# Four of six key/value chunks as seven half products instead of eight

## The reference

```
kv = rms_norm(x1, g_kv) @ w_kv      # 640 x 2048 by 2048 x 3072
k, v = jnp.split(kv, 2, axis=-1)    # outputs, and used by layer 1
```

## Time and profile before

| | us |
|---|---|
| three runs: median (lowest, highest) | 2202.61 (2198.36, 2204.11) |
| the profiled execution, and its span | 2199.25, 2197.6 |
| PE, DVE, ACT, POOL busy | 2166.1, 1140.8, 880.5, 314.8 |
| out_a starts / kv starts / in_b starts (first matmul) | 821.0 / 1045.4 / 1380.8 |

### The profile page before, as it was taken

One profiled execution on the slowest core, in us unless ns is written; L12 is line 12 of the kernel. 1 busy time (PEld: TensorE's weight loads), 2 busy tenths in 40 slices (PEclk: granted clock), 3 DMA queues, 4 the chain that ended last, 5 costly groups with the idle time before them and its releaser, 6 DMA issues.

```text
span 2197.6 us, 33765 instructions
## 1 busy us (share of the span) xinstructions
PE 2166.1 (99%) x12524; PEld 1860.4 (85%) x12524; DVE 1140.8 (52%) x1972; ACT 880.5 (40%) x1701; POOL 314.8 (14%) x466
## 2 busy tenths in 40 slices
PE   8999999999999999999999999999999999999998
PEld 6888888888888998888788888888888888988887
DVE  5758988988745463224522222255555554663223
ACT  5643333233455352222422222456565655542221
POOL 1622111211101000001100000113131322010000
PEclk9999999999999999999999999999999999999999
DMA  8734434534644334223433333444444445544224
GB/s 272 224 110 118 107 107 104 134 101 118 230 138 143 108 111 174 77 77 121 138 101 100 116 100 100 135 148 133 145 146 144 131 144 187 167 153 172 77 76 153
DMA packets 177399, 293.38 MB, mean 134 GB/s; under 512 B 25477, under 2 KB 105009, under 8 KB 174001
## 3 DMA queue, kind: packets, MB, share of 16 engines
q1 hardware_dynamic: 133872, 164.57, 24.5%
q0 software_dynamic: 24448, 87.68, 12.9%
q10 hardware_dynamic: 19008, 40.18, 5.3%
HBM read 243.09 MB, written 48.61 MB: 133 GB/s over the span
## 4 chain that ended last, share of the span: by engine, by line
PE 81%; DVE 11%; issue 3%; ACT 3%; DMA 2%; DVEq 0%; ACTq 0%; SPq 0%; POOL 0%
PE PS L1547 11%; PE PS L1549 11%; PE PS L1548 11%; PE PS L214 10%; PE PS L215 10%; PE PS L216 10%; PE PS L1509 2%; DVE WL L196 2%; PE PS L1511 2%; PE PS L1510 2%; PE PS L828 1%; DVE FA L659 1%; DVE FA L655 1%; ACT WH L182 1%; DVE FA L650 1%
## 5 line engine op out<-in xcount | busy, mean ns | idle before, releaser
L214 PE MATMUL PS<-XH,WH 128*128 128x512 f32 (+1 forms) x1408 | 522.7, 371 | 1.5 <-DVE EST L2294 1.5
L196 DVE SCALAR_TENSOR_TENSOR WL<-RAW,vec,WH 128x256 fp32r<-128x256 f32 (+1 forms) x608 | 281.4, 523 | 459.7 <-ACT WH L182 455.0
L215 PE MATMUL PS<-XL,WH 128*128 128x512 f32 (+1 forms) x1408 | 511.1, 363 | 0.0
L216 PE MATMUL PS<-XH,WL 128*128 128x512 f32 (+1 forms) x1408 | 510.5, 363 | 0.0
L1547 PE MATMUL PS<-WH,XH 128*128 128x512 f32 x1168 | 457.8, 392 | 7.3 <-DVE WL L196 4.2
L1549 PE MATMUL PS<-WH,XL 128*128 128x512 f32 x1168 | 455.6, 390 | 0.0
L1548 PE MATMUL PS<-WL,XH 128*128 128x512 f32 x1168 | 455.4, 390 | 0.0
L182 ACT ACTIVATE WH<-RAW,vec 128x256 fp32r<-128x256 f32 (+1 forms) x608 | 281.8, 533 | 336.9 <-DMA RAW<-in_w_kv_dram 172.1
L191 DVE TENSOR_TENSOR WL<-RAW,WH 128x1024 fp32r<-128x1024 f32 (+1 forms) x120 | 142.0, 1186 | 323.7 <-ACT WH L178 323.2
L216 PEld LDWEIGHTS PS<-XH,WL 128*128 128x128 f32 x1408 | 264.4, 188 | 38.1
L214 PEld LDWEIGHTS PS<-XH,WH 128*128 128x128 f32 x1408 | 264.9, 188 | 35.6 <-DVE EST L2294 2.1
(11 more groups left out here) (328 smaller groups left out, 2376.8 us busy)
## 6 DMA issues: line engine op xcount, KB each, us to landing
RAW<-in_w_in_a_dram SPq DMA_DIRECT2D x64, 512.0 KB, 4.3
RAW<-in_w_in_b_dram SPq DMA_DIRECT2D x64, 512.0 KB, 4.0
RAW<-in_w_kv_dram SPq DMA_DIRECT2D x48, 512.0 KB, 3.7
RAW<-in_w_out_a_dram SPq DMA_DIRECT2D x32, 512.0 KB, 3.7
RAW<-in_w_out_b_dram SPq DMA_DIRECT2D x32, 512.0 KB, 3.8
scratch_in_a<-EST ACTq DMA_DIRECT2D x32, 320.0 KB, 4.1
RAW<-in_w_glu_dram SPq DMA_DIRECT2D x24, 384.0 KB, 3.2
scratch_in_b<-EST ACTq DMA_DIRECT2D x26, 320.0 KB, 3.4
```

The costliest lines, as they stand in the source:

```text
L196: ins = eng.scalar_tensor_tensor(out=wview(WL, slot, ph)[:, kt, :], in0=wview(RAW, slot, ph)[:, kt, :], scalar=vec[:, g:g + 1], in1=wview( ...
L214: pe.matmul(acc, wh, xh, start=first, stop=False)
L215: pe.matmul(acc, wh, xl, start=False, stop=False)
L216: return pe.matmul(acc, wl, xh, start=False, stop=last)
```

## The change

Chunks 2 and 3 of `w_kv` become pair 0, chunks 4 and 5 pair 1 (a new phase `pairs`). For the 512 prompt tokens a pair is a product of a 2 x 2 matrix of blocks of activations (256 tokens by 1024 rows each) and one of weights (1024 rows by 512 columns, B11 to B22), computed by Strassen's scheme in Winograd's form: seven block products instead of eight. Each takes 4 units of 512 KB and 2 token tiles. T1 to T4 are sums of weight blocks. The 128 sample tokens keep the full product, done beside the B units (B12 serves them alone).

- Sums of weights: during `out_a`, 16 pieces (one k-tile of a pair) are loaded by POOL as four 256 KB blocks, one is scaled on ACT, four DVE operations combine them in place, and four stores go to scratch, from where SP loads the T units later. Two piece buffers take the place of RES 0 and 1, whose row loads follow the last piece.
- Sums of activations: 10 DVE operations over 2048 columns in kv chunk 1, then a high (ACT) and a low part (DVE) of four results, in the place of OUTROW. For that the stores of x1 move from `x1_root` to kv chunk 0, and the sums wait for them.
- Results are combined by ACT copies from PSUM into stages and DVE sums with other banks, then stored.
- POOL's masks and the keys of head 0 come after the last pair.
- Row tiles of x in the first stage are loaded in four quarters, one per unit.

```diff
-ROW_AT = (0, 5, 10, 15, 20)
+ROW_AT = [(max(5 * t - 1 + p, 0), t, p) for t in range(NT) for p in range(4)]
...
+HALF_K = KT // 2
+PAIR_COLS = ((2, 3), (4, 5))
+PAIR_UNITS = [(op, g) for op in ("B11", "B21", "T2", "T1", "T3") for g in range(4)]
+PAIR_UNITS += [(op, g) for g in range(4) for op in ("B22", "B12")] + [("T4", g) for g in range(4)]
+COMBINED = ("T1", "T2", "T3", "T4")
+COMBINE_AT = [3 + 4 * x // 3 for x in range(2 * HALF_K)]
...
-                ("kv", io["w_kv"], 2, RW, 16, 6, 8),
+                ("kv", io["w_kv"], 2, RW, 16, 2, 8),
+                ("pairs", io["w_kv"], 2, RW, 16, 2, len(PAIR_UNITS)),
...
+            def pair_products(pair):
+                ph, banks = phases["pairs"], pair_banks(pair)
+                ev, gm = 10 + 10 * pair, M_C + 8 * pair
+                def ready(op, i):
+                    if op == "B11":
+                        if pair == 0:
+                            pe.wait_ge(s_ev["kv"], 6 + i)
+                        else:
+                            pe.wait_ge(s_gm, M_C + 6)
...
+                    elif op == "T2":
+                        pe.wait_ge(s_fl, F_S + 2)
+                        pe.wait_ge(s_ev["kv"], ev + 1 + i)
+                    elif op == "T1":
+                        pe.wait_ge(s_fl, F_S + 1)
+                        pe.wait_ge(s_ev["kv"], 8 + i if pair == 0 else 19 + i)
...
+                left = {"B11": (XH, XL, 0, 0), "B21": (XH, XL, HALF_K, 0), "T4": (XH, XL, HALF_K, 2)}
+                left |= {op: (SH[:, j], SL[:, j], 0, 0) for op, j in (("T1", 0), ("T2", 1), ("T3", 2), ("B22", 3))}
+                into = {"B11": "B", "T2": "B", "T3": "B", "T4": "B", "T1": "C", "B21": "D", "B22": "D"}
+                for k, (op, g) in enumerate(PAIR_UNITS):
+                    U = pair_unit(pair, k)
+                    pe.wait_ge(s_wl, U + 1)
+                    pe.wait_ge(s_wh, U + 1)
+                    wh, wl = wview(WH, k % RING, ph), wview(WL, k % RING, ph)
+                    if op != "B12":
+                        xh, xl, k0, t0 = left[op]
+                        for i in range(2):
+                            if g == 0:
+                                ready(op, i)
+                            c = slice(P * (t0 + i), P * (t0 + i) + P)
+                            for kt in range(2):
+                                x = k0 + 2 * g + kt
+                                first = g == 0 and kt == 0 and op in ("B11", "T1", "B21", "B22")
+                                ins = three(pe, PS[:, banks[into[op]][i], :], xh[:, x, c], xl[:, x, c], wh[:, kt, :], wl[:, kt, :],
+                                            first, g == 3 and kt == 1, skip_group_check=True)
+                    if op[0] == "B":
+                        bank = 5 + int(op[2])
+                        if pair and g == 0 and op in ("B11", "B22"):
+                            pe.wait_ge(s_ev["kv"], 13 if op == "B11" else 18)
+                        for kt in range(2):
+                            x = 2 * g + kt + (0 if op[1] == "1" else HALF_K)
+                            ins = three(pe, PS[:, bank, :], XH[:, x, HEAD:TOK], XL[:, x, HEAD:TOK], wh[:, kt, :], wl[:, kt, :],
+                                        g == 0 and kt == 0 and op in ("B11", "B22"), g == 3 and kt == 1 and op in ("B21", "B12"))
+                    ins.then_inc(s_wu, 1)
...
+            def scale_piece(x):
+                act.wait_ge(s_gt[x % 2], 16 * MIXB // 2 + 128 * (x // 2) + 64)
+                g = phases["pairs"].gcol + x % HALF_K
+                act.activation(PIECE[:, x % 2, 1, :], PIECE[:, x % 2, 1, :], ACT.Copy, scale=vec[:, g:g + 1]).then_inc(s_gs, 1)
...
+                        if l == 0 and ph.upc * n + k in COMBINE_AT:
+                            scale_piece(COMBINE_AT.index(ph.upc * n + k))
...
+            def set_high(j):
+                act.wait_ge(s_gm, M_S + j + 1)
+                act.activation(SH[:, j], SUM[:, j], ACT.Copy).then_inc(s_fh, 1)
...
+            def pair_copies(pair):
+                ph, banks = phases["pairs"], pair_banks(pair)
+                ev, gm, st = 10 + 10 * pair, M_C + 8 * pair, 32 + 32 * pair
+                def copy(stage, bank):
+                    act.activation(stage, PS[:, bank, :], ACT.Copy).then_inc(s_ev["kv"], 1)
+                def store(stage, block, t):
+                    act.dma_start(pair_dst(pair, block, t), stage).then_inc(s_kvst[t], 16)
+                def done(k):
+                    act.wait_ge(s_wu, pair_unit(pair, k) + 1)
+                for k in range(ph.upc):
+                    ahead(split_high, act, ph, pair_unit(pair, k), k)
+                    if k == 4:
+                        done(3)
+                        for t in range(NT if pair == 0 else 2):
+                            act.wait_ge(s_kvst[t], st)
+                        for i in range(2):
+                            copy(ST1[:, i, :], banks["B"][i])
+                    elif k == 8:
+                        done(7)
+                        act.wait_ge(s_kvst[NT - 1], st)
+                        copy(STS[:, 0, :], 6)
+                    elif k == 9:
+                        act.wait_ge(s_ev["kv"], ev + 3)
+                        store(STS[:, 0, :], 0, NT - 1)
+                        act.wait_ge(s_gm, gm + 2)
+                        for i in range(2):
+                            store(ST1[:, i, :], 0, i)
...
+                    elif k == 28:
+                        done(27)
+                        copy(STS[:, 1, :], 7)
+                    elif k == 29:
+                        act.wait_ge(s_ev["kv"], ev + 8)
+                        store(STS[:, 1, :], 1, NT - 1)
+                        act.wait_ge(s_gm, gm + 8)
+                        for i in range(2):
+                            store(ST2[:, i, :], 1, i)
+                done(ph.upc - 1)
+                for i in range(2):
+                    copy(ST4[:, i, :], banks["B"][i])
+                for i in range(2):
+                    act.wait_ge(s_ev["kv"], ev + 9 + i)
+                    store(ST4[:, i, :], 0, 2 + i)
...
+            def combine_piece(x):
+                b11, b12, b21, b22 = (PIECE[:, x % 2, j, :] for j in range(4))
+                g1 = phases["pairs"].gcol + x % HALF_K
+                g1, g2 = vec[:, g1:g1 + 1], vec[:, g1 + HALF_K:g1 + HALF_K + 1]
+                stt = dve.scalar_tensor_tensor
+                dve.wait_ge(s_gs, MIXB + x + 1)
+                mine(stt(out=b22, in0=b22, scalar=g2, in1=b12, op0=ALU.mult, op1=ALU.subtract))
+                mine(stt(out=b12, in0=b11, scalar=g1, in1=b12, op0=ALU.mult, op1=ALU.subtract))
+                mine.wait()
+                mine(stt(out=b11, in0=b11, scalar=g1, in1=b22, op0=ALU.mult, op1=ALU.add))
+                mine.wait()
+                stt(out=b21, in0=b21, scalar=g2, in1=b11, op0=ALU.mult, op1=ALU.subtract).then_inc(s_gm, 1)
...
+            def set_sum(j):
+                o = SUM[:, j]
+                if j == 0:
+                    dve.wait_ge(s_x1st, 80)
+                    mine(tt(o, high(1, 0), high(1, 1), ALU.add))
+                    mine.wait()
+                    mine(tt(o, o, low(1, 0), ALU.add))
+                    mine.wait()
...
+            def set_low(j):
+                dve.wait_ge(s_fh, F_S + j + 1)
+                dve.tensor_tensor(SL[:, j], SUM[:, j], SH[:, j].bitcast(F32), ALU.subtract).then_inc(s_fl, 1)
+            for k in range(ph.upc):
+                ahead(split_low, dve, ph, ph.upc + ph.first + k, k)
+                if k < 4:
+                    set_sum(k)
+                else:
+                    set_low(k - 4)
+            def pair_sums(pair):
+                ph, banks = phases["pairs"], pair_banks(pair)
+                ev, gm = 10 + 10 * pair, M_C + 8 * pair
+                def add(stage, b, op):
+                    for i in range(2):
+                        dve.tensor_tensor(stage[:, i, :], stage[:, i, :], PS[:, banks[b][i], :], op).then_inc(s_gm, 1)
+                for k in range(ph.upc):
+                    ahead(split_low, dve, ph, pair_unit(pair, k), k)
+                    if k == 8:
+                        dve.wait_ge(s_wu, pair_unit(pair, 7) + 1)
+                        dve.wait_ge(s_ev["kv"], ev + 2)
+                        add(ST1, "D", ALU.add)
...
+            for pair in range(2):
+                pair_sums(pair)
...
-            pool.wait_ge(s_fl, F_B)
+            pool.wait_ge(s_fl, F_S)
             pool.dma_start(GB[:], io["g_post_a"].broadcast_to([P, D])).then_inc(s_gb, 16)
-            for t in range(NRES):
+            for t in range(2, NRES):
+                pool.dma_start(RES[t], x_rows(t)).then_inc(s_resd[t], 16)
+            def load_piece(x):
+                pair, kt = x // HALF_K, x % HALF_K
+                for j in range(4):
+                    row, col = (kt + HALF_K * (j // 2)) * P, PAIR_COLS[pair][j % 2] * RW
+                    pool.dma_start(PIECE[:, x % 2, j, :], io["w_kv"][row:row + P, col:col + RW]).then_inc(s_gt[x % 2], 16)
```

(84 more changed lines are left out.)

109 lines of the change are left out of this document (87 added, 22 removed).

## The result

The changed kernel takes **2209.96 us** (median of 6 runs, 2208.16 to 2210.81) against 2200.42 for the kernel before (6 runs, 2198.36 to 2204.11): a ratio of 1.0043, 95% interval 1.0033 to 1.0053. It is 0.4% slower. The forecast was 2180 with 2171 to 2194 as its range; the result lies outside, near the price that rival (1) named for a piece loop of 11.5 us (2213); that the loop would run over 10.8 us had been given a chance of only 0.05. The profiled executions have spans of 2208.3 and 2197.6 us, 10.7 apart, and stand for the medians well enough.

The account below looks back on a forecast made before the run. TensorE, busy 99% of the span, was taken to bound the kernel. Terms of -21.8 + 1.5 + 1.5 - 2.5 - 1 gave -22.3 us, from a median of 2202.6 to 2180 us, range 2171 to 2194.

Parts of the forecast that it names:

- rival (1): Piece loop sets out_a's pace: 2190 at 10 us a piece, 2213 at 11.5; chance 0.11 up to 10.8 us, 0.05 above.
- The step that failed: Piece loop in out_a: overlapping loads and stores take 8.3 us per piece, below the 9.07 us at which pieces are due.
- two chains: Piece loop in out_a: the DMA chain takes 8.3 us, load with scale and sums 8.1, both below the scheduled 9.07.
- Piece 3: On out_a's first chunk's last unit: loads land at 870, where 870.9 was the latest allowed.
- Matmuls: Pairs replacing plain chunks: 48 fewer matmuls per pair, 96 in all at 0.2267 us, -21.8 us.
- Pairs: Weight loads in the pair stage, in shorter units through a ring of 4 slots: +1.5 us, bounds 0 and 7.
- rival (2): Weight ring starves in the pair stage: about 2202 us if landings take 7 us, 2186 at 5.5; chance 0.12.
- the 5.5 named as a sign against the forecast: Pair stage: a load landing in over 5.5 us would show the forecast wrong.
- Piece loop and boundaries: Piece loop in out_a: +1.5 us of stalls, at the first chunk boundary; bounds 0 and 10.
- Stretch between the projections: Between out_a and kv, x1 stores moved away: shorter first wait and no half clock, -2.5 us; bounds 0 and -3.9.
- Rows in quarters: First stage, x loaded in 20 issues instead of 5: -1 us, from 2.0 us of PE waits.
- Copies, sums and keys: Pair-stage copies and sums, quarter sums in kv chunk 1, masks and keys in in_b: hidden, costing nothing.

Follow-up runs that it names:

- The experiment with the DMAs alone: The changed kernel with pieces neither scaled nor combined, each store waiting only for its piece's load: 11.47 us a round, 2177.71 us (one run).
- that with four slots: The changed kernel with four piece buffers instead of two, pieces neither scaled nor combined: rounds of 6.6 us at the mean, 2177.65 us (one run).

## Why the prediction was wrong

**The step that failed** is "2.1 MB plus 0.6 of weights at 400 GB/s 6.8 us, plus about 1.5 to start: 8.3 us per piece". The rate holds, though I read it too kindly: the earlier trace rows has 328 to 454 GB/s in the busy slices and not 406 to 454; their mean is 398. At the measured 254 GB/s a round of 11.27 us moves 2.86 MB, the piece's 2.10 and weights, which at 0.41 MB a us are 7.0 us of transfers, near the forecast's 6.8. The other 4.3 us are the start, the dip and the tail of each round (the one pause is 0.3 of them), for which I had 1.5 with nothing measured behind it. It was an estimate in the one sum where 0.8 us of margin decided. The experiment with the DMAs alone gives the period directly, 11.5 us at 261 GB/s, so 7.3 of transfers and 4.2 of the rest, and that with four slots shows that the 4 us vanish once a round may start before the last has landed. I had given each of two chains its length, and both were below 9.07; that the chains close into a ring (loads of x wait for stores of x-2, which are issued behind the loads of x-1; from 902 to 913 us a store took 6.5 us to land at the median, a load 3.2) I saw only as overlap.

The Trainium skill, "DMA: Bandwidth & Descriptors", Anatomy of one DMA, puts a fixed 2.0 us on a DMA of this path, most of it the receipt of the write. An estimate from it is 7.0 + 2.0 = 9.0 us a round, below the schedule's 9.07 and so without stalls. The runs show 4.2 to 4.3 and not 2.0. One DMA in place of four doesn't lessen it (11.56 us a round), which fits a cost of the round rather than of the single DMA.

**Rival (1)** had the mechanism and the formula: (11.27 - 9.07) x 15 less 4 is 29.0 us of stalls, against 25.0 in gaps. The half clock behind them, 1.3 us a boundary in the prediction and in none of its sums, was 2.8, 2.3 and 1.8: 6.9 us. The boundaries can be read by it as well. The second and third chunk have six pieces each, so from 879.62 to 1014.86 there are twelve pieces in 135.2 us, 11.27 each, where two chunks of matmuls take 108.8. What I got wrong is the chance. Piece 3 was forecast "just in time", its loads landing at 870; ACT had it at 875.07.

**By terms.** Matmuls: 96 fewer at 0.227, -21.8, right. Pairs: +1.5 forecast, with bounds of 0 and 7; the two windows last 197.5 us for 864 matmuls, which at 0.2267 are 195.9, so +1.6, the size forecast. No step between two starts there is over 0.4 us, no wait at B22 reaches 0.2 us, and rival (2) fell, though one load there took 5.7 us to land, over the 5.5 named as a sign against the forecast. Piece loop and boundaries: +1.5 forecast, 25.0 + 6.9 = +31.9 measured, the whole of the miss. Stretch between the projections: -2.5 forecast; in the trace of the change the first wait is 1.6 shorter and the half clock behind it (1.3) is gone, while a wait of 0.45 appears at 1078.40 and the later one grows from 1.09 to 2.62: -0.9 there, and nothing when tried alone. The sentence "The later wait hangs on a chain through the sample rows and may eat part" was right and should have been costed. Rows in quarters: -1 forecast; about -3 by the medians of one pair of kernels, and nothing in the change's own profile, where out_a starts 0.4 later than before: open. Copies, sums and keys: hidden, as forecast.

Seven other kernels that keep the whole change stand between 2177 and 2185 us, 14 to 24 below the kernel before in their groups, where the forecast was 22.3. So the rest of the sum was sound to some us; that 2180 itself comes out in three of them owes 2 us to luck, for it was set against a median of 2202.6 where six runs gave 2200.4. With one line of its schedule put otherwise (two slots, slower schedule) the change gives 2179.39.

## What to carry to other kernels

A load, compute, store loop over few slots is a ring: before counting bytes, write down which landing each issue waits for, and add the time in which the queue stands empty in each turn, taken from a trace of such a turn and not guessed. Here it was 4 us of 11.3, and two more slots removed it. If the loop can't be made faster, schedule its consumers at the pace it has, and put none of them just ahead of the work that frees a bank, because in-order engines turn a late piece into a stall of TensorE, which then comes back at half clock.
